# Time step of the first mixer in float32, from the raw inputs, in column groups of the array

## The reference

```python
h = h + ssd_retention_mixer(rmsnorm(h, mix_norm), *mix_params)
...
u = h @ w_in
z, xbc, dt_raw, q, k, v, g = split_cols(u, ...)        # dt_raw: 16 columns
...
xbc = jax.nn.silu(causal_dwconv(xbc, conv_w, conv_b)).astype(f32)
dt = jax.nn.softplus(dt_raw.astype(f32) + dt_bias.astype(f32))
a_dt = dt * (-exp(a_log));  a_cs = cumsum(a_dt)
```

## Time and profile before

| | us |
|---|---|
| median of the runs | 1741.71 |
| lowest, highest of 3 | 1741.26, 1742.13 |
| the profiled execution, its own time | 1741.78 |
| its span | 1740.1 |
| TensorE busy in it | 1726.4 (99%) |
| VectorE busy | 1184.5 (68%) |
| ScalarE busy | 772.7 (44%) |

### The profile page before, as it was taken

The page is one execution under the profiler, slowest core; times in us unless marked ns, Lnnn a source line. Parts: engine busy times, 40 slices in busy tenths (PEclk is TensorE's granted clock), DMA queues, the critical chain, the costliest instruction groups (busy, mean ns, idle before and its releaser), DMA issues.

```text
span 1740.1 us, 34423 instructions
## 1 busy us (share of the span) xinstructions
PE 1726.4 (99%) x13556; PEld 1654.1 (95%) x13556; DVE 1184.5 (68%) x1713; ACT 772.7 (44%) x1068; POOL 7.6 (0%) x35
## 2 busy tenths in 40 slices
PE   9999999999999999999999999999999999999998
PEld 7999999999999999999999899999989999999887
DVE  7888767658457887884334777777775788888333
ACT  5455443234434232322223777777874423233222
POOL 0000000000000000000000000000000000000000
PEclk9999999999999999999999999999999999999999
DMA  4322232222222323223223222222222223223322
GB/s 161 125 85 86 98 104 79 74 73 73 61 97 85 96 85 92 89 94 100 86 83 104 77 70 79 76 74 82 76 62 89 94 89 91 96 86 109 100 85 80
DMA packets 43889, 154.22 MB, mean 89 GB/s; under 512 B 5137, under 2 KB 8209, under 8 KB 43169
## 3 DMA queue, kind: packets, MB, share of 16 engines
q1 hardware_dynamic: 42064, 146.10, 26.9%
q10 hardware_dynamic: 1744, 6.99, 1.1%
HBM read 146.62 MB, written 2.13 MB: 85 GB/s over the span
## 4 chain that ended last, share of the span: by engine, by line
PE 93%; DVE 4%; ACT 2%; issue 1%; DMA 0%; SPq 0%; DVEq 0%; ACTq 0%
PE gp L461 81%; PE small L678 2%; PE small L558 1%; PE small L729 1%; PE small L596 1%; PE small L506 1%; PE gp L837 1%; PE small L740 1%; DVE wlo L1359 1%; PE small L496 1%; PE small L700 1%; ACT whi L867 0%; DMA hT<-in 0%; PE small L489 0%; PE small L696 0%
## 5 line engine op out<-in xcount | busy, mean ns | idle before, releaser
L461 PE MATMUL gp<-hn_hi,whi 128*128 128x256 f32 (+2 forms) x3200 | 658.4, 287 | 1.5 <-DVE wlo L1359 0.6
L461 PE MATMUL gp<-hn_hi,wlo 128*128 128x256 f32 (+2 forms) x3200 | 647.2, 283 | 0.0
L461 PE MATMUL gp<-hn_lo,whi 128*128 128x256 f32 (+2 forms) x3200 | 645.9, 283 | 0.0
L867 ACT ACTIVATE whi<-raw 128x1024 fp32r<-128x1024 f32 (+1 forms) x248 | 273.0, 1101 | 678.4 <-PE gp L461 677.8
L1359 DVE TENSOR_TENSOR wlo<-raw,whi 128x1024 fp32r<-128x1024 f32 (+1 forms) x248 | 316.2, 1275 | 316.3 <-ACT whi L867 316.0
L461 PEld LDWEIGHTS gp<-hn_hi,whi 128*128 128x128 f32 x3200 | 500.3, 188 | 5.6 <-issue 1.8
L461 PEld LDWEIGHTS gp<-hn_lo,whi 128*128 128x128 f32 x3200 | 498.0, 188 | 0.0
L461 PEld LDWEIGHTS gp<-hn_hi,wlo 128*128 128x128 f32 x3200 | 497.2, 188 | 0.0
L461 PE MATMUL gp<-hid_hi,wlo 128*128 128x256 f32 (+1 forms) x506 | 132.3, 318 | 0.0
L461 PE MATMUL gp<-hid_hi,whi 128*128 128x256 f32 (+1 forms) x506 | 132.3, 318 | 0.0
L461 PE MATMUL gp<-hid_lo,whi 128*128 128x256 f32 (+1 forms) x506 | 131.9, 317 | 0.0
(11 more groups left out here) (277 smaller groups left out, 1862.1 us busy)
## 6 DMA issues: line engine op xcount, KB each, us to landing
raw<-in SPq DMA_DIRECT2D x217, 512.0 KB, 3.6
raw<-in SPq DMA_DIRECT2D x32, 704.0 KB, 4.1
cs_bc<-cs_scratch ACTq DMA_DIRECT2D x4, 1056.0 KB, 6.1
q_turned<-qs SPq DMA_DIRECT2D x16, 132.0 KB, 4.2
k_turned<-ks SPq DMA_DIRECT2D x16, 132.0 KB, 4.2
hT<-in SPq DMA_DIRECT2D x3, 528.0 KB, 6.7
out<-yT SPq DMA_DIRECT2D x6, 256.0 KB, 2.6
rdec<-in ACTq DMA_DIRECT2D x1, 1056.0 KB, 6.3
```

The source lines that it names most:

```text
L461: ins = pe.matmul(psum[:, h, c0:c0 + n_cols], wp[w.par][:, cols], rp[:, k0 + k, q0:q0 + n_cols], start=first and k == 0 and n == 0, stop=l ...
L867: act.activation(whi[w.par][:, 0:kt * P], raw[w.par][:, 0:kt * P], ACT.Copy).then_inc(hi_done, 1)
```

## The change

The time step is no longer a unit. Its weights come alone, 32 columns of each tile (of which 16 count) into `dtw`, and VectorE multiplies them by the gain. TensorE multiplies them in plain float32 with the raw tiles of `hT`: 16 matmuls of 264 tokens, the eight tiles over four groups of 32 columns of the array, so that tiles 0 to 3 write to rows 0, 32, 64 and 96 of two spare banks and tiles 4 to 7 add to them. The first four stand ahead of unit 0, four behind its second tile, eight behind its fourth. ScalarE copies the sums to `dt_part`, and two float32 matmuls with `sel` (three unit matrices added) add the four groups, behind unit 2. There are 10 matmuls of zeros in place of 20.

Unit 0 is loaded ahead of tiles 2 to 7, and split between tiles 1 and 2. Unit 2 goes to the spare banks 2 and 3 of `small`; the sum of squares moves from unit 1 to unit 2 (`k == 1`), and unit 3's split ahead of the root. VectorE evacuates units 0, 1 and 2 first, one behind the other (a third and a fourth input of the convolution lie in `dec`), and the first group's convolutions, time step and splits follow in a new order. The turning to tokens moves from behind unit 3 into unit 5 (`k == 2`). The numbers of units and pairs move by one, since a unit is gone.

```diff
-ZEROS_AHEAD = 20
+ZEROS_AHEAD = 10
@@ SyncE @@
                 if c == 0:
-                    unit(At(0, 0, 0), w_dt[0])
-            unit(At(0, 0, 1), w_ssd[0])
+                    sp.dma_start(dtw[:], w_dt[0].rearrange("p (k c) -> p k c", c=P)[:, :, 0:DT_ROWS]).then_inc(dtw_in, 16)
+                if c == 1:
+                    unit(At(0, 0, W_SSD), w_ssd[0])
@@ TensorE @@
-            zeros_ahead(ZEROS_AHEAD)
-            gemm(At(0, 0, W_DT), At(0, 0, T_DT), hn_hi, hn_lo, ready=(nlo_done, 0), psum=sp_[0:SSD_HEADS, 2:4, :],
-                 width=SSD_HEADS)
+            def dt_products(ks):
+
+                for k in ks:
+                    if k in H_FIRST:
+                        pe.wait_ge(h_in[H_FIRST[k]], 16)
+                for h in range(2):
+                    for k in ks:
+                        rows = slice(DT_ROWS * (k % DT_GROUPS), DT_ROWS * (k % DT_GROUPS + 1))
+                        ins = pe.matmul(sp_[rows, 2 + h, 0:H2], dtw[:, k, :], hT[:, k, h * H2:(h + 1) * H2],
+                                        start=k < DT_GROUPS, stop=k >= DT_GROUPS, skip_group_check=True)
+                if ks[-1] == KD - 1:
+                    ins.then_inc(dtp_done, 1)
+
+            def dt_between(k):
+                if k == 1:
+                    dt_products((2, 3))
+                if k == 3:
+                    dt_products((4, 5, 6, 7))
...
+            zeros_ahead(ZEROS_AHEAD)
+            pe.wait_ge(dtw_done, 1)
+            dt_products((0, 1))
+            gemm(At(0, 0, W_SSD), At(0, 0, 0), hn_hi, hn_lo, ready=(nlo_done, 0), after=dt_between)
+            hgemm(At(6, 0, W_SSD + 1), At(0, 0, 1))
+            pe.wait_ge(dtcopy_done, 1)
+            gemm(At(6, 0, W_SSD + 2), At(0, 0, 0), hn_hi, hn_lo, psum=sp_[:, 2:4, :], after=norm_first)
+            pe.wait_ge(normln_done, 1)
+            pe.wait_ge(sel_done, 1)
+            for h in range(2):
+                ins = pe.matmul(sp_[0:SSD_HEADS, h, 0:H2], sel[:], dt_part[:, h * H2:(h + 1) * H2], start=True, stop=True)
+            ins.then_inc(dtsum_done, 1)
+            for c in range(3, 6):
+                hgemm(At(6, 0, W_SSD + c), At(6, 0, T_SSD + c), after=dt_turned if c == 5 else None)
             pe.wait_ge(dtok_done, 1)
@@ ScalarE @@
-            split_hi(At(0, 0, 1))
+            split_hi(At(6, 0, W_SSD + 1))
             for m in range(KD):
                 square(0, m, m % 2)
+                if m == 1:
+                    act.wait_ge(dtp_done, 1)
+                    act.activation(halves(dt_part), sp_[:, 2:4, 0:H2], ACT.Copy).then_inc(dtcopy_done, 1)
                 if m == 4:
-                    split_hi(At(6, 0, W_SSD + 1))
-            split_hi(At(6, 0, W_SSD + 2))
+                    split_hi(At(6, 0, W_SSD + 2))
+            split_hi(At(6, 0, W_SSD + 3))
             inverse_root(0)
@@ VectorE @@
+            ve.wait_ge(dtw_in, 16)
+            ve.tensor_tensor(dtw[:], dtw[:], vec[:, 0:KD].unsqueeze(2).to_broadcast([P, KD, DT_ROWS]),
+                             ALU.mult).then_inc(dtw_done, 1)
...
+            for c in range(3):
+                first_tile(c)
+            split_lo(At(6, 0, W_SSD + 4))
+            dt_in()
+            first_conv(0)
+            first_tile(3)
+            split_lo(At(6, 0, W_SSD + 5))
+            dt_sums()
+            first_conv(1)
+            ssd_tile(0, 4)
+            split_lo(At(6, 0, W_SSD + 6))
+            first_conv(2)
+            dt_tokens()
+            first_conv(3)
```

More of the change, by code:

```diff
@@ L233, in build @@
                 aexp = sb("aexp", [SSD_HEADS, 1], f32, s1)
+                dtw = sb("dtw", [P, KD, DT_ROWS], f32, s1)
+                sel = sb("sel", [P, SSD_HEADS], f32, s1)
+                dt_part = dec[1][:, 0:T]
+                conv_in = (ub[:, 0, :], ub[:, 1, :], dec[2][:, 0:3 + T], dec[3][:, 0:3 + T])
             with scope() as s2:
@@ L914, in _ @@
             ch.link(act.activation(nspt[:], pcol("lru_lam", 0, 8), ACT.Abs))
+            split_hi(At(6, 0, W_SSD + 4))
             act.wait_ge(dtx_done, 1)
@@ L918, in _ @@
             ch.link(act.activation(dtl, dtl, ACT.Exp, scale=-1.0))
-            split_hi(At(6, 0, W_SSD + 3))
             act.activation(dtl, dtl, ACT.Ln, bias=1.0).then_inc(dtl_done, 1)
@@ L975, in decay @@
                 act.activation(e[0:SZ[4], FULL:CAUSAL], e[0:SZ[4], FULL:CAUSAL], ACT.Exp).then_inc(e_done, 1)
-            for c in range(1, 5):
-                if c > 1:
-                    split_hi(At(6, 0, W_SSD + c + 2))
-                if c == 2:
-                    act.wait_ge(cs_done, 1)
-                    act.dma_start(cs_d, csr).then_inc(cs_out, 16)
-                if c == 3:
-                    act.wait_ge(cs_out, 16)
-                    load_bc(0)
+            split_hi(At(6, 0, W_SSD + 5))
+            act.wait_ge(cs_done, 1)
+            act.dma_start(cs_d, csr).then_inc(cs_out, 16)
+            split_hi(At(6, 0, W_SSD + 6))
+            act.wait_ge(cs_out, 16)
+            load_bc(0)
             ssd_silu(0)
@@ L1381, in inverse_root @@
                 ve.wait_ge(rstd_done, n + 1)
-            def dt_cols(w):
-                return w[:, 0:KD * P].rearrange("p (k c) -> p k c", c=P)[:, :, 0:SSD_HEADS]
             def evacuate(w, t, dst, scale=None, t0=0):
@@ L1417, in _ @@
                 if m == 1:
-                    ve.wait_ge(hi_done, 1)
-                    ve.tensor_tensor(dt_cols(wlo[0]), dt_cols(raw[0]), dt_cols(whi[0]).bitcast(f32),
-                                     ALU.subtract).then_inc(lo_done, 1)
-            split_lo(At(0, 0, 1))
+                    split_lo(At(0, 0, W_SSD))
+            split_lo(At(6, 0, W_SSD + 1))
             for m in range(KD):
@@ new lines, in first_conv, with dt_tokens @@
+            def first_conv(c):
+                if c == 2:
+                    ve.wait_ge(third_done, 1)
+                else:
+                    t = At(0, 0, c) if c < 2 else At(6, 0, T_SSD + c)
+                    ve.wait_ge(pair_free[t.par], t.half + 1)
+                ct = c if c < 2 else (8 if c == 2 else 12)
+                conv(xcv[:, c, :], conv_in[c], 4, lambda k: pcol("ssd_cw", 4 * ct + k), pcol("ssd_cb", ct),
+                     ch.link, conv_done)
+            def dt_tokens():
+                ve.wait_ge(dtT_done, 1)
+                for n, (dst, sign) in enumerate(((dt_tok, 1.0), (ncs_tok, -1.0))):
+                    ve.tensor_scalar(dst[:, 0:4, :], sp_[:, 2, 80 * n:80 * n + 64].rearrange("p (i h) -> p i h", h=16),
+                                     sign, None, ALU.mult)
+                    ins = ve.tensor_scalar(dst[0:SZ[4], 4, :], sp_[0:SZ[4], 2, 80 * n + 64:80 * n + 80], sign, None,
+                                           ALU.mult)
+                ins.then_inc(dtok_done, 1)
@@ new lines, in _ @@
+            for c in range(3):
[12 more added lines that the diff above has]
+            first_conv(3)
+            for e in range(2):
+                rows = slice(HEAD * e, HEAD * (e + 1))
+                ve.tensor_copy(dcol[rows, :], vec[rows, COLS["ssd_d"] + e:COLS["ssd_d"] + SSD_HEADS:2])
```

68 lines of the change are left out of this document (29 added, 39 removed).

## The result

| | us |
|---|---|
| before, median of 22 runs | 1741.65 |
| changed, median of 22 runs | 1743.98 (1743.12 to 1744.80) |
| ratio | 1.0013, interval 1.0007 to 1.0019 |
| the changed kernel's profiled execution, its own time | 1743.12 |
| its span | 1741.2 |

The kernel became slower by 2.3 us in 1742, clear of the scatter and within the 0.2% (3.5 us) that the text on record calls no change. The forecast was 1743.3. One run of the kernel before, among the 33 taken beside e1 to e4, took 2808.61 us; it is left out of the ratios, and nothing on record explains it.

The account below looks back on a forecast made before the run. TensorE, busy 1726.4 of 1740.1 us, was taken as the bound. VectorE's chain put unit 7 at 60.75 in place of 59.18, 1.6 us later: 1743.4 against the profiled 1741.78, 1743.3 for the median, range 1739.3 to 1747.3.

Parts of the forecast that it names:

- The bound, and the place: TensorE's work sets the time; the opening puts unit 7 1.6 us later, and nothing behind it changes that.
- The start of unit 0: On TensorE, 10.25 in place of 14.71: weights land at 7.9, 1.5 us of it for dtw's load, then both splits.
- from 1.5 us on with the clock down: Price of dtw's load from which the kernel was said to be slower than before; above 0.2% from about 3.4 us.
- The float32 products: Twelve matmuls inside unit 0, overlapping in column groups: 2.55 us, between 1.8 and 6.1.
- The cost of going in and out: Extra time at each of the two float32 blocks inside unit 0: 0.4 us each, 1.8 in all without it.
- The clock: TensorE falls to 1.2 GHz around unit 0's start for 3.0 us, losing 1.5; rival that it stays up: 0.22.
- The chain behind it: From the sum of squares over VectorE's 27.2 us of work and 2.0 of pauses to unit 7 at 60.75.
- S: Start of the sum of squares on TensorE, behind two tiles of unit 2: 27.6, before 22.89.
- TensorE's own way: Unit 7 at about 59.8 if VectorE did not set it; as a rival 1738.5 to 1741 us, chance 0.10.
- The paragraph on the point of the sum: Root found 5.87 us of TensorE's work further on, with 30 us of VectorE's work behind it, only 2 in hand.
- no overlap: Rival: float32 products in unit 0 run one behind another, 5.3 + 0.8 us in place of 2.55; 1745 to 1747.5, chance 0.11.
- a dear load: Rival: dtw's load costs 5.7 us in place of 1.5, unit 0 4.2 later; 1744.5 to 1750 us, chance 0.14.

Follow-up runs that it names:

- e1: Changed kernel with 20 zeros matmuls in place of 10, and 12 more between the first float32 products and unit 0: 1741.74 us, 0.9998 of before.
- e4: Changed kernel with VectorE's split of unit 7 between the decay arguments of the first group's two heads: 1743.29 us, 1.0010 of before.
- e6: Changed kernel with the time step's weights packed in memory, so dtw loads as 128 pieces of 1 KB, not 1024 of 128 bytes: 1744.82 us, 1.0014 of before.
- e9: Changed kernel with the edits of e1, e4, e5 and e6 together and a new VectorE order: 1741.72 us, 0.9998 of before.
- e3: Changed kernel with all eight tiles of the float32 products in one group of 32 columns in place of four: 1745.66 us, 1.0023 of before.
- e2: Changed kernel with 20 zeros matmuls in place of 10 and none added between the first float32 products and unit 0: 1742.03 us, 1.0003 of before.
- e7: Changed kernel with the edits of e1 and e4 together: 1742.00 us, 0.9998 of before.
- after_again1: Changed kernel unedited, profiled a second time: own time 1744.46 us, unit 7 at 61.50.
- after_again2: Changed kernel unedited, profiled a third time: own time 1744.55 us, unit 7 at 61.61.
- e5: Changed kernel with the sum of squares behind the seventh tile of unit 1, not the second of unit 2: 1743.90 us, 1.0012 of before.
- e10: e5 with unit 2 back in the pair gp0 in place of the spare banks: 1750.31 us, 1.0051 of before.

## Why the prediction was right, point by point

**The bound, and the place.** The time followed unit 7's start: from there to the end of the profiled executions' own time it is 1682.6 and 1682.7 us before, 1682.65 to 1683.0 in the three of the changed kernel. That nothing behind unit 7 gives back or adds held to 0.4 us. That the time ahead of it came out within 0.3 us in the first trace is in part luck, as the next points show.

**The start of unit 0.** 9.82 for 10.25 in the first trace, 9.90 and 11.00 in the others. The weights were in use at 7.45 in the first trace and at 7.44 to 8.63 over the ten with the load in pieces, around the forecast's 7.9. But the reason was not the right one: the text charged the size of the pieces to unit 0's weights, and packing the load (e6, e9) doesn't bring them forward. The rule of the Trainium skill (DMA: Bandwidth & Descriptors, Specifications) that a transfer below 512 bytes misses the line rate agrees in its direction with the load itself, which lands after 3.2 to 4.2 us in pieces and after 2.7 and 2.8 packed; no effect of it on unit 0's start can be seen. The sentence on record that this load makes the kernel slower "from 1.5 us on with the clock down" is a slip: by the text's own sum that holds with the clock up, and with the clock down the kernel is slower at any price of the load.

**The float32 products.** Forecast 2.55, measured 2.0 at the higher clock (e1: 11.76 to 12.77 and 14.44 to 15.47). The 2.52 of the first trace agree by luck, for 0.5 of them are the clock's, which has its own term. The choice by the earlier trace rows, that halves overlap and so quarters do, is shown by e3. The cost of going in and out was too high: the sum had 0.4 for each block, and e1's first block has 0.13 (1.01 less two times 0.44). (The 28 records of the earlier trace rows have 5440 columns by the kernel's loops and not 5376; nothing hangs on the 1%.)

**The clock.** The step that carried the sign. It was low in unit 0, and e1 gives it back. The term was mis-sized: 1.5 us on record, 1.7, 2.6 and 1.6 measured. The row taken was the three us that the zeros need, from one trace; others show up to 4.8 (e2, e7: 1.23 to 6.06), and in after_again1 the lower level lasted 6 us behind unit 0's start. The text let the clock come up under ten zeros and fall again, and in the first trace it may not have come up at all. Unit 7 is 0.75 later than forecast in after_again1, by the clock, and 0.86 later in after_again2, mostly by the start of unit 0; which of the two makes the 0.7 us between the forecast and the median is not shown. Against the profiled execution's 1743.12 the forecast's 1743.4 is 0.3 high.

**The chain behind it.** Pauses 1.7 for 2.0, unit 7 at 60.47 for 60.75, S (the sum of squares) at 27.25 for 27.6. In S three errors meet: unit 0 began 0.4 early, products and clock together took 3.7 for 4.05, and the units themselves took 13.7 from unit 0's start to S (e1: 15.76 less 2.04) where the text had 13.3. VectorE does set unit 7 (e4), and TensorE's own way was 0.7 us shorter, where the text had about 1.

**The paragraph on the point of the sum was wrong in one half.** It laid the loss to the root that is found further on. e5 moves the sum of squares ahead and nothing changes: what VectorE's chain hangs on is the end of unit 2, whose evacuation the new order puts ahead of everything else. The sum had that pause in it; the sentence drew the wrong moral from it.

**The chances.** The clock's fall had no chance of its own but stood in the forecast; the two slow rivals, no overlap and a dear load, are both shut out, by e3 and by unit 0's start at 9.82 to 11.00 us. The slow side outside 0.2% was given 0.21, more than the rows bear with hindsight, because no row showed groups of 32 columns or small pieces.

## What to carry to other kernels

An engine that bounds the time is not sped up by an earlier start if the start leaves it idle in bursts: the matmuls of zeros ahead of the work were cut with the wait that they had filled, and the clock took 2.2 us (the changed kernel against e1), which turned no change into a small loss. A wait costs more than its length when the clock goes down with it: e10's wait of 4.8 us in the middle of the work cost 6.3. Before work is pulled forward on one engine, count what the second engine has in hand at the next place where the two meet; here VectorE had 2 us in hand, and with every repair that was tried (e9) unit 7 starts only 0.5 us earlier than before. And a value that is found later costs nothing as long as the first thing that uses it waits for something else, which an order of instructions shows and a dependence doesn't.
